# Two rows of a weight slab laid side by side: one packet of 8192 bytes for a partition in place of two of 4096

## The reference

```python
def reference(x, p, positions, ...):
    h = x
    for i in range(DEPTH):                                   # DEPTH = 2
        h = h + token_mixer(rms_norm(h, norm_mix_g[i]), positions, w_in[i], ..., w_o[i])
        h = h + peer_ffn(rms_norm(h, norm_ffn_g[i]), peer_w_query[i], peer_sub_keys[i], peer_u[i], peer_v[i])
        h = h + per_layer_embedding(h, p[i], w_ple[i], ple_norm_g[i], w_ple_gate[i])
    return rms_norm(h, final_norm_g)

def peer_ffn(...):    # for a chunk of 128 tokens
    q = (xc @ w_query).reshape(c, PEER_HEADS, 2, half)
    scores = jnp.einsum('chpd,hpnd->chpn', q, sub_keys)
    # top 16 of 128 in each half, top 16 of the 256 sums: 8 heads x 16 experts for each token
    u = expert_u[ids]
    pre = jnp.einsum('chkd,cd->chk', u, xc)
    act = gate * jax.nn.gelu(pre, approximate=False)
    return jnp.einsum('chk,chkd->cd', act, expert_v[ids])

def per_layer_embedding(h, p_i, w_ple, ple_norm_g, w_ple_gate):
    gate = jax.nn.sigmoid(rms_norm(h, ple_norm_g) @ w_ple_gate)
    return gate * (p_i @ w_ple)
```

## Time and profile before

| | |
|---|---|
| median of three runs | 1773.37 us |
| span of the profiled execution | 1769.8 us |
| total of the profiled execution | not given apart from the span |
| PE busy | 79% of the span |
| VectorE busy | 60% |
| GpSimd busy | 33% |
| ScalarE busy | 25% |
| bytes moved | 624.41 MB, 353 GB/s over the span |
| mean granted TensorE clock | 0.901 of full speed |

### The profile page before, as it was taken

How to read it: one execution, slowest core, us unless ns; L and a number is a source line. 1 busy time by engine, 2 the same in 40 slices (tenths; PEclk the granted TensorE clock), 3 DMA queues, 4 the chain that set the end, 5 groups by cost and what they waited for, 6 DMA issues and landing times.

```text
span 1769.8 us, 13794 instructions
## 1 busy us (share of the span) xinstructions
PE 1402.4 (79%) x4300; PEld 710.9 (40%) x4300; DVE 1063.0 (60%) x2683; ACT 441.2 (25%) x1406; POOL 587.8 (33%) x516
## 2 busy tenths in 40 slices
PE   7985579987669886899578896889867788877777
PEld 6662245453224453446223363445422333333332
DVE  3569855568975535565996533666698454454444
ACT  0412244121222224421212213431212221222222
POOL 0012334433343333434333331344243344344430
PEclk9987889999779998899888998899988989788989
DMA  8347988999889997899989997899988999989992
GB/s 336 120 158 311 372 329 324 420 378 390 323 342 403 398 418 308 332 415 418 398 331 361 377 416 306 332 378 410 418 354 321 379 376 399 409 346 418 394 381 119
DMA packets 94405, 624.41 MB, mean 353 GB/s; under 512 B 10112, under 2 KB 10624, under 8 KB 28800
## 3 DMA queue, kind: packets, MB, share of 16 engines
q0 software_dynamic: 73728, 536.90, 75.9%
q1 hardware_dynamic: 20608, 86.68, 12.5%
HBM read 622.49 MB, written 1.05 MB: 352 GB/s over the span
## 4 chain that ended last, share of the span: by engine, by line
PE 42%; DVE 25%; DMA 22%; ACT 7%; issue 3%; POOL 2%; ACTq 0%; DVEq 0%; POOLq 0%
PE acc L493 29%; DMA ring<-in_rows,ids 22%; DVE ring L988 10%; PE bank L737 2%; ACT act_w L813 2%; PE bank L786 2%; PE bank L527 2%; POOL ring L468 2%; DVE wb L1258 1%; ACT diag L818 1%; PE bank L645 1%; PE bank L532 1%; ACT L810 1%; DVE top_i L1265 1%; DVE top_i L1256 1%
## 5 line engine op out<-in xcount | busy, mean ns | idle before, releaser
L493 PE MATMUL acc<-ring,diag 128*128 128x512 f32 x2048 | 1010.9, 651 | 327.0 <-ACT diag L818 326.9
L468 POOL DMA_INDIRECT ring<-in_rows,ids x512 | 587.6, 1148 | 1139.5 <-PE acc L493 981.0
L988 DVE CUSTOM_DVE_ANT_0 ring<-ring,xc 128x1024 f32<-128x1024 f32 x512 | 613.2, 1223 | 436.3 <-DMA ring<-in_rows,ids 434.6
L493 PEld LDWEIGHTS acc<-ring,diag 128*128 128x128 f32 x2048 | 419.1, 210 | 891.8 <-issue 497.4
L810 ACT ACTIVATE gel<-pre 128x4 f32<-128x4 f32 (+1 forms) x134 | 27.5, 205 | 966.7 <-DVE pre L988 966.5
L818 ACT ACTIVATE diag<-cst,act_w 128x128 f32<-128x128 f32 x512 | 164.3, 390 | 4.4
L813 ACT ACTIVATE act_w<-gate,gel 128x1 f32<-128x1 f32 (+1 forms) x512 | 109.6, 283 | 6.0
L645 PE MATMUL bank<-wring,hT 128*128 128x512 f32 x128 | 56.7, 593 | 0.8 <-DVE hT L1211 0.8
L786 PE MATMUL bank<-wring,hT 128*128 128x512 f32 x128 | 56.5, 593 | 0.3 <-DVE hT L1025 0.3
L810 ACT ACT_TABLE_LOAD x20 | 25.7, 1283 | 115.4 <-DVE pre L988 115.4
L737 PEld LDWEIGHTS bank<-hT,wring 128*128 128x128 f32 x384 | 44.0, 192 | 2.4 <-issue 2.4
(11 more groups left out here) (234 smaller groups left out, 1000.1 us busy)
## 6 DMA issues: line engine op xcount, KB each, us to landing
wring<-in_w_out SPq DMA_DIRECT2D x16, 1024.0 KB, 12.1
wring<-in_w_gate SPq DMA_DIRECT2D x16, 1024.0 KB, 11.6
wring<-in_w_in SPq DMA_DIRECT2D x16, 978.0 KB, 8.7
wring<-in_w_query SPq DMA_DIRECT2D x12, 1024.0 KB, 11.4
ring<-in_rows,ids POOLq DMA_INDIRECT x512, 9.3
ring<-in_w_in SPq DMA_DIRECT2D x8, 978.0 KB, 14.8
wring<-in_w_ple SPq DMA_DIRECT2D x4, 1024.0 KB, 11.3
wring<-in_w_latent SPq DMA_DIRECT2D x4, 768.0 KB, 10.3
```

The costliest lines, as they stand in the source:

```text
L468: pool.indirect_dma_start(out=ring[:, n % RING, :], out_offset=None, in_=rows, in_offset=bass.IndirectOffsetOnAxis(ap=ids[:, w % 2, k:k + ...
L493: last = pe.matmul(acc[:, c, :], diag[:, j, :], ring[:, j, D + c * 512:D + c * 512 + 512], start=False, stop=True, skip_group_check=True)
L988: dve.tensor_tensor_reduce(out=u, in0=u, in1=xc[:, step % 2, :], scale=1.0, scalar=0.0, op0=ALU.mult, op1=ALU.add, accum_out=pre[:, j:j + ...
```

## The change

The four weights are rearranged in memory before the kernel starts, so that rows p and 128 + p of a slab stand next to each other, and the load of a slab has one run of 8192 bytes for each partition. What lands in the slot is the same, byte for byte, and nothing that reads it changes.

```diff
-                "out": lambda l, k: w_out[l, 2 * k * P:2 * (k + 1) * P, :].rearrange("(a p) n -> p a n", p=P),
-                "query": lambda l, k: w_query[l, 2 * k * P:2 * (k + 1) * P, :].rearrange("(a p) n -> p a n", p=P),
-                "gate": lambda l, k: w_gate[l, 2 * k * P:2 * (k + 1) * P, :].rearrange("(a p) n -> p a n", p=P),
-                "ple": lambda l, k: w_ple[l].rearrange("(a p) n -> p a n", p=P),
+                "out": lambda l, k: w_out[l, k],
+                "query": lambda l, k: w_query[l, k],
+                "gate": lambda l, k: w_gate[l, k],
+                "ple": lambda l, k: w_ple[l, k],
...
-                    load(held[:].rearrange("p (a n) -> p a n", a=2), source["query"](l, 0), held_in)
+                    load(held[:], source["query"](l, 0), held_in)
...
-                if len(src.shape) == 3:
-                    dst = wring[:, n % WRING, :].rearrange("p (a n) -> p a n", a=2)
-                else:
-                    dst = wring[:, n % WRING, 0:src.shape[1]]
-                sp.dma_start(dst, src).then_inc(weight_in[n % WRING], 16)
+                sp.dma_start(wring[:, n % WRING, 0:src.shape[1]], src).then_inc(weight_in[n % WRING], 16)
...
+    def pairs_of_rows(w):
+        w = np.asarray(w)
+        return w.reshape(DEPTH, -1, 2, P, D).transpose(0, 1, 3, 2, 4).reshape(DEPTH, -1, P, 2 * D)
...
-        "w_out": np.asarray(w_o),
-        "w_query": np.asarray(peer_w_query),
+        "w_out": pairs_of_rows(w_o),
+        "w_query": pairs_of_rows(peer_w_query),
...
-        "w_ple": np.asarray(w_ple),
-        "w_gate": np.asarray(w_ple_gate),
+        "w_ple": pairs_of_rows(w_ple),
+        "w_gate": pairs_of_rows(w_ple_gate),
```

## The result

| | before | after |
|---|---|---|
| median of 20 runs each | 1775.49 us (1764.27 to 1788.82) | 1787.03 us (1772.07 to 1798.47) |
| ratio after to before | | 1.0063, 95% interval 1.0041 to 1.0085 |
| span of the profiled execution | 1769.8 us | 1793.5 us |

The change makes the kernel slower by 0.63%, 11.5 us. No change was forecast, 1771.1 us within 1763 to 1783; the time lies above the range.

What follows compares the result with a forecast made beforehand. No engine is full; gather landings bound the kernel, sharing the DMA engines with weights. Term 1's 2.3 us and term 2's 0 take the span from 1769.8 to 1767.5; plus 3.6 gives 1771.1 us, range 1763 to 1783.

Steps and rivals of the forecast that it cites:

- The ring of waits: GpSimd waits 981.0 us for PE's slots, VectorE 434.6 us for gathered rows; behind VectorE come ScalarE and PE again.
- Term 1, the service of a byte: Larger packets on the weight queue save 0.085 us of DMA service for one load; 2.3 us come off the span.
- the 27 loads in full stretches: Loads where the DMA share is 0.96 or more; each saves 0.085 us, together 2.3 us off the span.
- Term 2, the share: Weights take about half the bandwidth beside gathers; a gather lands 1.1 us later; -13 to +13 us, taken as 0.
- the twelve loads that were counted in stretches with gaps: Loads where DMA has idle time; each moves a gather's landing by up to 1.1 us, later or sooner.
- The rival on the slower side: At 12 loads in stretches with gaps, waited-for gathers land 1.1 us later, not caught up: +11 us, 1784 us; chance 0.17.
- The rival on the faster side: At the same 12 loads, waited-for gathers come behind the load and find it finished earlier: -15 us, 1758 us; chance 0.16.
- That packets stay as they are: Weight packets are still cut at 4096 bytes in the issue, so nothing changes: 1773 us; chance 0.03.
- SP's queue: SP, held 10.66 us issuing its first three output loads, may be through sooner; costed at 0, at most 10 us.

Runs made afterwards that it cites:

- e12: Weight-ring loads after the first step's bring only 1024 of a partition's bytes, so PE multiplies mostly leftover weights; ratio to the kernel before 0.9861.
- e9: New layout with 1024-byte packets for output, query, gate and embedding loads, 1956-byte for input slabs; ratio to the kernel before 0.9939, 1765.54 us.
- e2: The changed kernel's layout, but padded so that each partition's load goes in two packets of 4096 bytes; ratio to the kernel before 1.0011.
- e3: The changed kernel's layout, padded so that each partition's load goes in four packets of 2048 bytes; ratio to the kernel before 0.9983.
- e11: New layout with output loads in 2048-byte packets, input slabs in 1956, query, held, gate and embedding loads in 8192; ratio to the kernel before 1.0014.
- e1: The changed kernel again, no edit, in a second set of runs beside the kernel before; ratio 1.0077.
- e7: The changed kernel with twelve embedding and gate loads held back until PE has released more ring slots; ratio to the kernel before 1.0104.

## Why the prediction was wrong

**What bounds the kernel:** half right. The ring of waits is the one described, and the gathers' landing is the wait through which the change acts. "A microsecond of DMA service is worth a microsecond" in full stretches is wrong. e12 took away 120 us of service for 25, and e9 added 27 us and won 10. The burst followed above lies in a stretch with a share of 1.01, and there the change costs time.

**Term 1, the service of a byte:** its size was right (about 4 us less over the span, where 50 loads at its 0.085 us come to 4.3), its worth was not. No run shows the 2.3 us of the 27 loads in full stretches.

**Term 2, the share:** the mechanism was right. Four stretches of 6 us in this burst in which both queues have work all through: the kernel after and e2 at 801.4 to 807.4 us, e3 at 780 to 786, e9 at 779.5 to 785.5:

```profile
q0 software_dynamic: 172, 1.26, 50.7%
q1 hardware_dynamic: 167, 1.25, 49.5%
...
q0 software_dynamic: 218, 1.63, 65.5%
q1 hardware_dynamic: 213, 0.86, 35.7%
...
q0 software_dynamic: 276, 2.00, 79.0%
q1 hardware_dynamic: 275, 0.55, 23.5%
...
q0 software_dynamic: 304, 2.23, 88.4%
q1 hardware_dynamic: 302, 0.30, 14.1%
```

Packet stands beside packet each time, so the gathers get 50%, 65%, 78% and 88% of the bytes at 8192, 4096, 2048 and 1024. The time falls in the same order: 1.0063, 1.0011 (new layout), 0.9983, 0.9939 (the last with small input packets as well), though neighbours among the last three overlap or differ in more than one thing. Over longer stretches the shares say less: in the 12 us from the burst the kernel after moves 3.03 MB of gathers and e2 3.04, because in both there are 2 us in which hardly any gather has bytes left to move (0.07 and 0.06 MB beside 0.79 and 0.77 of weights).

The step that failed is this one: "In a full stretch this is worth nothing over the whole: gathers have moved as many bytes when the four loads are through", and with it the 0 that term 2 was given. In its place the runs show a loss in a full stretch that is not made up there. In the burst of the third step (the table above) the gather that is waited for lands after 18.5 to 20.7 us and not 16.1 to 17.2, the bandwidth behind it falls to 341 to 375 GB/s where it was 413 to 419, just when the gathers should have caught up, and PE is through half of the query product after 44.5 to 49.6 us and not 40.7 to 44.1. The whole change costs 11.5 us. The prediction charged 1.1 us, for one gather, and took the middle of plus and minus where the sum was one-sided.

How the share becomes this delay is not worked out. Four gathers queued up at 1.1 us each would be 4.4 us, near the 2.3 and 3.3 measured, but the bytes don't bear that sum out: over the whole wait the gathers have the same share in both kernels, 59.4% before (783.94 to 800.08 us) and 59.2% after (794.46 to 813.93), and in the longer wait more bytes of both queues pass, 4.82 and 3.40 MB against 4.01 and 2.74.

Two readings behind this step were off as well. PE needs not two matmuls for a gather but four (2048 for 512 gathers), 7.13 / 4 = 1.8 us at the full clock, which leaves it less room to catch up at 2.5 us a gather. And three of the twelve loads that were counted in stretches with gaps, the gate loads at 396 us, stand in a full one (share 1.02, 418 GB/s at 396 to 420 us).

**The rival on the slower side** gave 1784 us, near the 1787.03 measured, with its mechanism: the gather that is waited for stands beside the burst, and the time is not caught up. Its place was wrong: it charged only 12 loads in stretches with gaps, output loads above all, and e11 and the burst show the cost at other loads, in full stretches. So its number, 11 us beside 11.5, is in part luck. It had a chance of 0.17. **The rival on the faster side,** that later gathers find the queue free sooner, does not show in any ratio: the kernel with 8192-byte packets is slower than each one with smaller ones throughout. **That packets stay as they are** is ruled out by the packet count.

**SP's queue:** right to cost nothing. SP issues the first three output loads in 6.38 us and not 10.66, and nothing follows from it.

The rule on arbitration that the prediction took from the Trainium skill ("DMA: Bandwidth & Descriptors", Queues, rings and completion order) should have weighed more than the one on a packet's fixed cost: both hold here in kind, but only the first is seen to reach the critical path. By the page an engine drains a packet of several descriptors before it turns to the next queue; the traces show only that equal numbers of contiguous runs pass from both queues, from 8192 down to 1024 bytes (the packet counts above). By term 1 the order of the four sizes would have been the reverse of the one measured.

**What stays open.** Which loads cost how much: 0.6 and 0.3 us for a load are not apart. Where the rest of the 11.5 us is lost: only the burst of the third step was followed, and it shows some 3 us. How much is PE's clock: it was granted 0.75 behind the burst above. Over all recorded executions its mean is 0.896 in the 20 of the change and 0.898 in the 6 of e1, against 0.900 in the 29 of the kernel before beside e1; 0.4% of PE's 1402 us is an estimate of 6 us at most, and whether that is a cause or a consequence of the longer waits no run here shows. And whether e7's 8 us in the choice of experts are a loss over the change as a whole; its ratio to it, taken from two sets, is 1.0041 with intervals that overlap.

## What to carry to other kernels

In this kernel the packet size of the queue that nobody waits for set how much it took from the one that is waited for, while both had work. Where two queues share the DMA engines like this, try prefetches in smaller packets than the urgent transfers, until they begin to land too late. Fewer and larger packets save service (about 4 us here), but service was not what the path was made of; the packets of the gathers themselves were not varied. A DMA share near 1 does not show that bytes bound the stretch: take bytes away and see.

## What the hardware showed that was not expected

1024-byte packets on a queue beside 8192-byte ones cost it 27 us more service over the span (14.1% against 12.5%), and the gathers' median landing hardly moved (9.5 us against 9.3). VectorE's wait for them was 417.8 us in that execution, against 434.6 and 446.6 in two kernels with 4096-byte packets (before and e2) and 436.8 and 454.0 in two executions of the change; the four kernels with query packets of 2048 bytes or less have 417.8 to 426.7, below all others that compute everything. Two executions of the same kernel (the change) are already 7 us apart at the first query load of the second step, 335.91 and 328.92 us.
